# Softmax maxima from products over 128 rows instead of 64

## What is computed

```python
def attend(q, k, v):                 # block 1, swept in blocks of queries
    s = jnp.einsum("bqkgd,btkd->bkgqt", qi, k).astype(jnp.float32)
    w = jax.nn.softmax(s, axis=-1).astype(v.dtype)
    return jnp.einsum("bkgqt,btkd->bqkgd", w, v)

def diff_attention(q, k, v, lam):    # block 2, causal
    sc = jnp.einsum('bchqd,bchkd->bchqk', ...) * scale
    p = jax.nn.softmax(jnp.where(mask, sc, -jnp.inf), axis=-1)
    w = p[:, 0] - lam * p[:, 1]
```

## Time and profile before

| | |
|---|---|
| timed runs | 3411.47 us median of 3 (3408.11, 3411.47, 3420.42) |
| profiled execution | span 3422.3 us; the page gives no other time of it |
| busy share of the span | PE 92%, PEld 73%, DVE 59%, ACT 30%, POOL 29% |
| instructions | 38543, of which PE 15388 products and as many weight loads |
| mean granted PE clock | 0.954 of full speed |
| chain that ended last | PE 39%, DVE 6%, ACT 2%, POOL 2%, issue 2% of the span |

### The profile page before, as it was taken

One profiled execution on the slowest core, in us unless ns is written; L12 is line 12 of the kernel. 1 busy time (PEld: TensorE's weight loads), 2 busy tenths in 40 slices (PEclk: granted clock), 3 DMA queues, 4 the chain that ended last, 5 costly groups with the idle time before them and its releaser, 6 DMA issues.

```text
span 3422.3 us, 38543 instructions
## 1 busy us (share of the span) xinstructions
PE 3136.8 (92%) x15388; PEld 2496.7 (73%) x15388; DVE 2032.0 (59%) x3032; ACT 1030.7 (30%) x1799; POOL 1005.8 (29%) x754
## 2 busy tenths in 40 slices
PE   6998999999999999989899998899989888989798
PEld 3985667888488888879565675688869856777576
DVE  4566765555665555573576554666665845667344
ACT  3125763000231111141366201322231135421352
POOL 1003765553210000010277585100000325531262
PEclk9999999999999999999899999999999978999799
DMA  6411003333322112123101565232222210122100
GB/s 203 156 53 28 10 29 93 105 105 114 111 74 74 50 74 74 50 91 108 28 1 38 145 169 194 83 106 93 91 69 78 101 41 1 44 75 95 49 1 25
DMA packets 206354, 267.76 MB, mean 78 GB/s; under 512 B 29297, under 2 KB 133697, under 8 KB 205537
## 3 DMA queue, kind: packets, MB, share of 16 engines
q1 hardware_dynamic: 204096, 265.30, 24.1%
q10 hardware_dynamic: 2080, 0.01, 0.0%
HBM read 254.65 MB, written 10.52 MB: 77 GB/s over the span
## 4 chain that ended last, share of the span: by engine, by line
PE 39%; DVE 6%; ACT 2%; POOL 2%; issue 2%; DMA 1%; SPq 0%; DVEq 0%; POOLq 0%
PE ps L373 14%; PE ps L2010 5%; PE ps L2020 4%; PE ps L2500 2%; PE ps L1329 2%; PE ps L1792 1%; PE ps L1312 1%; PE ps L2830 1%; PE ps L1282 1%; PE ps L2775 1%; PE ps L1094 1%; PE ps L3184 0%; DVE U L2945 0%; PE ps L2789 0%; DVE U L1439 0%
## 5 line engine op out<-in xcount | busy, mean ns | idle before, releaser
L752 POOL TENSOR_TENSOR ht_lo<-HT,ht_hi 128x1024 fp32r<-128x1024 f32 x28 | 67.7, 2418 | 1077.4 <-DVE X L710 629.7
L2010 PE MATMUL ps<-ht_hi,w_hi 128*128 128x512 f32 (+1 forms) x832 | 286.6, 344 | 18.5 <-POOL ht_lo L752 9.8
L2010 PE MATMUL ps<-ht_lo,w_hi 128*128 128x512 f32 (+1 forms) x832 | 285.2, 343 | 0.0
L2010 PE MATMUL ps<-ht_hi,w_lo 128*128 128x512 f32 (+1 forms) x832 | 285.1, 343 | 0.0
L2020 PE MATMUL ps<-w_hi,a_hi 128*128 128x512 f32 x640 | 252.2, 394 | 4.3 <-DVE a_lo L2135 4.3
L2020 PE MATMUL ps<-w_lo,a_hi 128*128 128x512 f32 x640 | 251.1, 392 | 0.0
L2020 PE MATMUL ps<-w_hi,a_lo 128*128 128x512 f32 x640 | 250.7, 392 | 0.0
L373 PE MATMUL ps<-w_lo,ht_hi 128*128 128x320 f32 (+2 forms) x800 | 244.6, 306 | 0.0
L1496 POOL TENSOR_TENSOR p_lo<-ring,p_hi 128x512 fp32r<-128x512 f32 x156 | 200.1, 1293 | 116.2 <-DVE p_hi L1451 88.3
L595 DVE SCALAR_TENSOR_TENSOR U<-U,stat 128x512 f32<-128x512 f32 x224 | 219.9, 982 | 12.0 <-DMA U<-w_ada_dram 2.0
L373 PE MATMUL ps<-gate_ht_hi,gate_w_hi 128*128 128x512 f32 (+1 forms) x576 | 212.8, 369 | 11.7 <-POOL w_lo L1678 6.4
(11 more groups left out here) (427 smaller groups left out, 8293.4 us busy)
## 6 DMA issues: line engine op xcount, KB each, us to landing
ring<-w_dram SPq DMA_DIRECT2D x30, 2048.0 KB, 7.9
U<-w_ada_dram SPq DMA_DIRECT2D x80, 512.0 KB, 3.6
ring<-w_in_dram SPq DMA_DIRECT2D x48, 512.0 KB, 6.5
ring<-w_in_dram SPq DMA_DIRECT2D x8, 1280.0 KB, 5.9
ring<-a_w_in_dram SPq DMA_DIRECT2D x8, 1280.0 KB, 6.7
ring<-w_ada_dram SPq DMA_DIRECT2D x4, 2048.0 KB, 10.6
hi_scratch<-ht_hi SPq DMA_DIRECT2D x2, 3072.0 KB, 10.0
gate_ht_hi<-hi_scratch SPq DMA_DIRECT2D x8, 768.0 KB, 4.5
```

Of the source, the lines that this page charges most:

```text
L752: pool.tensor_tensor(HT_LO[:, :, tokens], HT[:, :, tokens], HT_HI[:, :, tokens].bitcast(F32), ALU.subtract).then_inc(ht_ready.sem, 1)
L2010: last = pe.matmul(ps[:, g % 4, 0:c1 - c0], lhsT, rhs, start=(k + j == 0), stop=(k == KD - 1 and j == 2))
```

## The change

In both `maximum` functions, every product of a softmax with 64 features takes all 128 rows of its two operands in place of rows 0 to 63: k_hi and k_lo against q_hi twice. Numbers of products, columns, banks, waits and signals stay. MLA heads keep their 96 rows, and the mask's product stays as it is.

```diff
@@ -1274,7 +1274,7 @@
                         past(pe, j_split, js_0, piece_at[h + 1])
                         past(pe, m_taken, mt_0, n)
                         past(pe, n_taken, nt_0, h)
-                        d = QK if mla(h) else HD
+                        d = QK if mla(h) else P
                         q, k = QH[h % HB], KH[kbuf(h)]
@@ -2783,10 +2783,10 @@
                         if jobs[c].mem:
                             for i in range(2):
                                 t = 2 * m + i
-                                last = pe.matmul(ps[:, 0, i * M:(i + 1) * M], q[0:HD, t * P:(t + 1) * P], k[0:HD, 0:M],
+                                last = pe.matmul(ps[:, 0, i * M:(i + 1) * M], q[:, t * P:(t + 1) * P], k[:, 0:M],
                                                  start=True, stop=True)
                         else:
-                            pe.matmul(ps[:, 0, 0:(m + 1) * P], q[0:HD, m * P:(m + 1) * P], k[0:HD, 0:(m + 1) * P],
+                            pe.matmul(ps[:, 0, 0:(m + 1) * P], q[:, m * P:(m + 1) * P], k[:, 0:(m + 1) * P],
                                       start=True, stop=False)
```

## The result

The changed kernel takes 3382.8 us (median of 4 runs, 3378.8 to 3386.5) against 3410.5 us before (4 runs, 3408.1 to 3420.4). The ratio is 0.9916, with a 95% interval of 0.9898 to 0.9934: by the ratio 28.6 us less (22.5 to 34.8), from median to median 27.7. The forecast was 33.5 us less.

The account below looks back on a forecast made before the run. PE was taken to bound three of four stretches, a chain of waiting steps the fourth. Block 1's 18, block 2's 15 and 0.5 sum to 33.5 us, from 3411.5 to 3378 us; range 3355 to 3402.

Parts of the forecast that it names:

- The gap of 0.38 us and its cause: Around each 64-row maximum on PE: two drains from changing the tiling mode, 0.38 us together, absent with 96 rows.
- Rival (C): The gap comes from the pair itself, not its rows, so 128 rows change nothing: 3411.5 us; chance 0.05.
- the 0.60 of the sum: Block 2's softmaxes at clock 0.5: gap of 0.60 us, from 1.23 us less the columns' time.
- block 2's gross: Block 2, first layer, before waits: 20.5 us from 46 maxima plus 2.4 from the chain at the start, gross 23.
- 128 rows cost nothing more than 64: Products of the maxima: columns set the pace, so 128 rows against 64 were costed at nothing.
- Block 1, 18 us: GQA heads' 72 maxima: 24.5 us gross, 12 if the turn's wait grew to the MLA heads'; 18 taken, half way.
- Block 2, 15.5 us: Block 2's softmaxes: 15 us in the first layer, between 8 and 23, and 0.5 in the second, between 0 and 4.8.
- the 60% in it: Block 2, first layer: share taken of the 20.5 us gross outside the starting chain, the remainder going to waits for DVE.
- Clock: PE's falls to 1.2 GHz, about 5 us lost each: no change in number counted, two more or one less in the range.
- Rival (D): Longer PE stops bring more clock falls; seven eat the gain, ten or eleven give 3431 us; chance 0.07.
- Stretches: Block 1's GQA heads: the stretch in layer 2 some 8 us shorter, in layer 1 some 10.

Follow-up runs that it names:

- e4_second_64: Changed kernel with the second product of each maximum's pair in block 1's GQA heads back at 64 rows; ratio 0.9941 to the kernel before.
- e11_fewer_casts: Changed kernel, maxima's turn one unit later (block 1) and behind the values (block 2), one rounding per block 1 head from DVE to ACT; 0.9854, 3363.1 us.

## Why the prediction was right

The forecast was 33.5 us less, the result is 28.6 (22.5 to 34.8), inside the range. Step by step:

- **The gap of 0.38 us and its cause.** Right: 0.81 and 0.41 us in place of 1.21 and 0.79, 65 rows do the same as 128, and a 64-row product put elsewhere brings the gap with it. Rival (C) is out. At clock 0.5 the gap is 0.49 us and not the 0.60 of the sum, which takes 46 x 0.3 x 0.11 = 1.5 us off block 2's gross.
- **128 rows cost nothing more than 64.** Right; 65 and 128 rows take the same time.
- **Block 1, 18 us** between 12 and 24.5. Measured alone 15.7 timed, 18.3 in the stages of the changed kernel. The wait at the turn grew as forecast, to 8.4 / 7 = 1.2 us a head in layer 2 (forecast 1.2 to 1.8). The step that was missed is a second taker: PE now also waits for DVE's reduce ahead of the next maximum, so a unit takes 1.69 us where I had 1.53, and L1282's "issue" went from 28 to 16 times and not away, where the prediction's signs had it nearly vanish. My 18 was half way between two bounds and not worked out; that it came within 3 us is in part luck.
- **Block 2, 15.5 us.** Measured alone 16.7. L2796's wait grew by more than "a little" (13.7 to 21.6 us). The profiled stage shows 18 to 20 us, part of it clock: against the same stage at 0.85 (178.2 us), the 128 rows at 0.84 to 0.85 (164.7 to 167.3 us in six profiles) are worth 11 to 14 us. So the term was of the right size, and the clock moves it by several us either way; the 60% in it was a choice too.
- **Clock.** No more falls: behind block 2's start, slices of 4 us show five or six before and five or six now. The granted clock rose from 0.80 to 0.84 in block 2 and from 0.95 to 0.97 in layer 1 of block 1. Rival (D) found nothing. The longest stop, 3.29 us at L2796, was followed by products 0.43 us apart for under 3 us.
- **Stretches.** Forecast 8 us shorter in layer 2 of block 1 and 10 in layer 1; 6.9 and 11.4 measured.

The forecast's surplus of 5 us is of the size of the measurement's interval, and I can't assign it to one term. The wait that I missed in block 1 and the low-clock gap that I had too large both point that way.

## What to carry to other kernels

Look at starts, not durations, around products with 64 rows among larger ones (fewer rows were not tried): where the weight load of such a product, and the next larger one's, waits for "issue", some 0.38 us a visit can be had by taking 65 or more rows, if the rows hold something harmless or useful. Runs of such products should stand together, since a pair costs what one costs. "Issue" alone is no proof, though: here it also hid a wait for DVE to empty the two banks, so compare its end with the end of that work. And move the steps that wait for another engine's short answer (here the turned maxima) behind independent work. In block 1 this was worth 20 us in the kernel before, without the change, and 13 us on top of it.

## What the runs showed of the hardware

- A 64-row product among larger ones costs 0.38 us at clock 1.0 for entry and exit together, with 65 rows none (0.82 us for four products that take 1.21 around a 64-row pair); at clock 0.5 it was 0.49 us (0.74 against 1.23); one or two such products in a row cost the same (1.20 and 1.21 us for the same four products). For a short product of 64 columns it was 0.31 us.
- The 65-row and the 64-row loads take nearly the same time (191 and 188 ns on average); what differs is that the 64-row load doesn't start beside the running product (held 0.36 us in e4_second_64).
- A producer and a consumer that share one pair of PSUM banks alternate: 0.59 us of products and 0.96 us of DVE's reduce gave 1.69 us from one start to the next, though both engines waited in between (0.68 and 0.73 us in e11_fewer_casts).
- The same instructions of block 2's softmaxes took 185.7 us at a mean granted clock of 0.80 and 178.2 us at 0.85 in another profile, with no change in that stage; no run shows why. Such a difference, 7.5 us, is a quarter of the whole effect here.
